# A two-model kernel on one core: the experts' head and end rearranged, and the feed-forward loops cut at another place

## The reference

```python
x = x + 0.5 * swiglu_ffn(rms_norm(x, ffn1_norm[l]), w_gate, w_up, w_down)   # d_ff 2816
...                                                                          # retention + attention
x = x + 0.5 * swiglu_ffn(rms_norm(x, ffn2_norm[l]), w_gate, w_up, w_down)
...
h = rmsnorm(x, g_ffn)                      # second block, after its mixer
g_prob = softmax(h @ w_rg + b_rg)          # 4 groups; the best one is taken
e_sel = (h @ w_re + b_re)[group]           # 8 experts in it; the best two are taken
y = sum over the two: combine * (silu(h @ w_gate[e]) * (h @ w_up[e])) @ w_down[e]
x = x + y
```

## Time and profile before

| | us |
|---|---|
| three runs | 1663.36, 1663.58, 1661.0 |
| median | 1663.36 |
| profiled execution | 1662.88 |
| its span, first to last instruction | 1661.0 |
| TensorE busy | 1503.5 |
| VectorE busy | 1006.8 |
| ScalarE busy | 701.3 |
| mean granted clock of TensorE | 0.955 |

### The profile page before, as it was taken

How to read it: one execution, slowest core, us unless ns; L and a number is a source line. 1 busy time by engine, 2 the same in 40 slices (tenths; PEclk the granted TensorE clock), 3 DMA queues, 4 the chain that set the end, 5 groups by cost and what they waited for, 6 DMA issues and landing times.

```text
span 1661.0 us, 28423 instructions
## 1 busy us (share of the span) xinstructions
PE 1503.5 (91%) x10855; PEld 1165.0 (70%) x10856; DVE 1006.8 (61%) x1859; ACT 701.3 (42%) x1211; POOL 70.1 (4%) x88
## 2 busy tenths in 40 slices
PE   8999999999999999999999999999988666666765
PEld 6888888788888888888788889888844323233322
DVE  6777788677777777787677777977643112222212
ACT  5555566455555555566455556746310000000000
POOL 1000030000001000030300000001000000000000
PEclk9999999999999999999999999999989888888788
DMA  9665363365654655363466545444889999999997
GB/s 312 202 202 177 111 240 127 102 221 184 196 183 154 212 177 193 124 239 101 144 206 202 177 152 177 154 153 149 322 353 428 429 428 428 427 428 429 429 429 320
DMA packets 152071, 407.81 MB, mean 246 GB/s; under 512 B 5568, under 2 KB 99120, under 8 KB 139344
## 3 DMA queue, kind: packets, MB, share of 16 engines
q1 hardware_dynamic: 150672, 404.28, 65.6%
q0 software_dynamic: 1344, 2.80, 0.7%
HBM read 406.00 MB, written 1.05 MB: 245 GB/s over the span
## 4 chain that ended last, share of the span: by engine, by line
PE 66%; DMA 22%; DVE 7%; ACT 3%; issue 2%; SPq 0%; DVEq 0%; ACTq 0%
DMA expert_gu<-in_exp_gu 22%; PE bank L2032 19%; PE bank L2038 10%; PE bank L1991 9%; PE bank L1992 9%; PE bank L1993 9%; PE bank L2623 3%; DVE wlo L1212 2%; ACT whi L767 1%; PE bank L2639 1%; DMA raw<-in_ffn_w_up 1%; PE bank L2576 1%; PE bank L2601 0%; DVE small L1355 0%; PE bank L2430 0%
## 5 line engine op out<-in xcount | busy, mean ns | idle before, releaser
L1212 DVE TENSOR_TENSOR wlo<-raw,whi 128x1024 fp32r<-128x1024 f32 (+1 forms) x396 | 449.6, 1183 | 80.3 <-ACT whi L767 80.2
L767 ACT ACTIVATE whi<-raw 128x1024 fp32r<-128x1024 f32 (+1 forms) x396 | 382.6, 1020 | 71.9 <-PE bank L1993 70.1
L2032 PE MATMUL bank<-hboth,whi 128*128 128x512 f32 x1408 | 350.3, 391 | 2.1 <-DVE hboth L1255 1.3
L2032 PEld LDWEIGHTS bank<-hboth,whi 128*128 128x128 f32 x1408 | 258.7, 188 | 54.0 <-ACT whi L767 2.0
L2623 PE MATMUL bank<-expert_gu,h_e 128*32 128x256 f32 x2112 | 170.1, 480 | 117.4 <-DMA expert_gu<-in_exp_gu 113.4
L2623 PEld LDWEIGHTS bank<-expert_gu,h_e 128*32 128x32 f32 x2112 | 77.0, 132 | 206.7 <-issue 117.6
L2038 PEld LDWEIGHTS bank<-hboth,wlo 128*128 128x128 f32 x1408 | 191.3, 190 | 13.1
L2038 PE MATMUL bank<-hboth,wlo 128*128 128x256 f32 x1408 | 196.0, 283 | 0.0
L1931 DVE SCALAR_TENSOR_TENSOR e_sg<-e_th,bank 128x128 f32<-128x128 f32 x33 | 9.5, 288 | 299.0 <-ACT e_th L1171 299.0
L1991 PE MATMUL bank<-whi,hboth 128*128 128x512 f32 (+2 forms) x384 | 150.3, 392 | 1.5 <-DVE hboth L1255 0.9
L1991 PE MATMUL bank<-whi,act_hi 128*128 128x512 f32 x352 | 140.1, 398 | 10.0 <-DVE act_lo L1321 10.0
(11 more groups left out here) (377 smaller groups left out, 1753.8 us busy)
## 6 DMA issues: line engine op xcount, KB each, us to landing
expert_gu<-in_exp_gu SPq DMA_DIRECT2D x62, 2048.0 KB, 40.4
expert_dn<-in_exp_dn SPq DMA_DIRECT2D x31, 2048.0 KB, 41.1
raw<-in_ffn_w_gate SPq DMA_DIRECT2D x44, 1024.0 KB, 5.5
raw<-in_ffn_w_up SPq DMA_DIRECT2D x44, 1024.0 KB, 7.5
raw<-in_ffn_w_down SPq DMA_DIRECT2D x44, 1024.0 KB, 4.9
raw<-in_w_in SPq DMA_DIRECT2D x36, 1024.0 KB, 5.2
raw<-in_w_o SPq DMA_DIRECT2D x8, 1024.0 KB, 5.4
raw<-in_w_out SPq DMA_DIRECT2D x4, 1024.0 KB, 5.0
```

The costliest lines, as they stand in the source:

```text
L767: nc.scalar.activation(slot_view(whi, slot, src), src, ACT.Copy).then_inc(hi_ready, inc)
L1212: nc.vector.tensor_tensor(slot_view(wlo, slot, src), src, slot_view(whi, slot, src).bitcast(F32), ALU.subtract).then_inc(lo_ready, inc)
L2032: nc.tensor.matmul(out_[:], wh[:, k, :], hboth[:, k, :, :], start=k == 0, stop=False, skip_group_check=True)
```

## The change

Feed-forward stages: on ScalarE and VectorE the split of a window's down weight moves from the head of the window to the end of the window before it, so the loops turn at another place; the first one stands ahead of the stage's row scale. On TensorE the row scale's two products stand ahead of the high products of window 1's gate instead of behind them. The branch for a feed-forward stage at the very end of the plan goes.

Experts' head: the router's columns become the weights and the tokens the moving data; the two halves of the result are copied to `logitsT` (one by ScalarE, one by VectorE) and turned back by TensorE. ScalarE takes over one of two copies of turned x. The norm product of the second half of x moves behind the logits' copy. `take` of the first block is made straight from the counts. The total counts go to another bank with a signal of their own. `rows(0)` and `rows(1)` move into the first block, behind its first half and ahead of its last two steps. The first three experts are written out ahead of the loop. `Y` is opened by products of the identity with x instead of zeros.

Experts' end: for experts 30 and 31 the scatters and the gather stand between the two halves of gate-up. Each bank of `Y` signals by itself, and is copied into x, two by VectorE and two by ScalarE. x is stored in four transfers instead of two.

```diff
+                for h in range(2):
+                    if not moe:
+                        sp.wait_ge(x_ready, 4 * len(stages) - 2 * (T - 1 - t))
+                    elif h == 0:
+                        sp.wait_ge(x_ready, 4 * len(plan) + t + 1)
+                    else:
+                        sp.wait_ge(xn_ready, 2 * T + t + 1)
+                    sp.dma_start(out[0, t * P:(t + 1) * P, h * 512:(h + 1) * 512], x[:, t, h * 512:(h + 1) * 512]).then_inc(stored, 16)
...
             def ffn(i):
                 st, b, m = plan[i]
                 base = 22 * kind_index(i)
-                row_scale(i)
+                def down_split(c, o, r):
+                    k = o // 2
+                    split_hi(st, (b + k) % 2, batch_value(b + k, r), 2, o % 2, m + 3 * c, m + 3 * o)
...
-                    split_hi(st, (b + k) % 2, batch_value(b + k, r), 2, o % 2, m + 3 * c, m + 3 * o, 3 if tail else 1)
...
+                    if o < 21:
+                        down_split(c + 1, o + 1, r)
+                down_split(0, 0, 0)
+                row_scale(i)
...
-                    for h in range(2 if t == 0 else 0):
+                    for h in range(2 if t == 0 else 1):
...
+                act.wait_ge(logits_done, 1)
+                nc.scalar.activation(logitsT[0:LOGITS, 0:P], bank[6][0:LOGITS, 0:P], ACT.Copy).then_inc(logits_copied, 1)
...
+                for t in range(T):
+                    act.wait_ge(y_ready, ends_of(i) + 2 * t + 2)
+                    nc.scalar.activation(x[:, t, 512:1024], Y[2 * t + 1][:], ACT.Copy).then_inc(xn_ready, 1)
...
+                def down_split(c, o):
+                    split_lo(st, (b + o // 2) % 2, 2, o % 2, m + 3 * c, m + 3 * o)
...
+                    down_split(c + 1, o + 1)
+                down_split(0, 0)
                 dve.wait_ge(rcol_ready, rcol_index(i) + 1)
...
+                dve.wait_ge(logits_done, 2)
+                V.tensor_copy(logitsT[0:LOGITS, P:S], bank[7][0:LOGITS, 0:P]).then_inc(logits_copied, 1)
+                dve.wait_ge(x_ready, 4 * i)
+                V.tensor_tensor(xn[:, 1, :], x[:, 1, :], gain[:], ALU.mult).then_inc(xn_ready, 1)
                 dve.wait_ge(root_ready, roots[0])
-                dve.wait_ge(logits_done, 1)
+                dve.wait_ge(logits_done, 3)
...
                 dve.wait_ge(counts_done, 1)
-                link(V.tensor_scalar(blocks[:, 0, :], bank[5][:, 2 * NE:3 * NE], 1.0, (BS - 1) / 2, ALU.max, ALU.add))
+                before_me = bank[5][:, 0:T * NE].rearrange("p (t n) -> p t n", t=T)
+                V.tensor_tensor(hits[:, 0:T, :], iota.rearrange("p (o s) -> p o s", o=1).broadcast_to([P, T, BS]),
+                                before_me[:, :, 0:1].broadcast_to([P, T, BS]), ALU.is_equal).then_inc(take_step, 1)
+                dve.wait_ge(take_step, 1)
+                V.tensor_tensor(take[:], hits[:, 0:T, :], both[:, :, 0:1].broadcast_to([P, T, BS]), ALU.mult).then_inc(take_ready, 1)
+                dve.wait_ge(counts_done, 2)
+                link(V.tensor_scalar(blocks[:, 0, :], bank[7][:, 0:NE], 1.0, (BS - 1) / 2, ALU.max, ALU.add))
...
-                update_x(i, 1.0)
+                for t in range(T):
+                    dve.wait_ge(y_ready, ends_of(i) + 2 * t + 1)
+                    V.tensor_copy(x[:, t, 0:512], Y[2 * t][:]).then_inc(x_ready, 1)
...
                         out_ = (G_, U_)[e][o % 2]
+                        if scale and e == 0:
+                            row_scale(i)
                         pe.wait_ge(lo_ready, mm + 1)
                         for k in range(KC):
                             high_product(out_, wh, k)
-                        if scale and e == 0:
-                            row_scale(i)
                         low_products(out_, wl, mm, 1)
...
+                        ins = nc.tensor.matmul(bank[6 + t][0:LOGITS, 0:P], w_router[:, k, :], hcol[:, k, t * P:(t + 1) * P],
+                                               start=k == 0, stop=k == KC - 1)
+                    ins.then_inc(logits_done, 1)
+                pe.wait_ge(logits_copied, 2)
+                for t in range(T):
+                    ins = nc.tensor.transpose(bank[4][:, t * LOGITS:(t + 1) * LOGITS], logitsT[0:LOGITS, t * P:(t + 1) * P],
+                                              ident[0:LOGITS, 0:LOGITS])
...
+                for t in range(T):
+                    for h in range(2):
+                        nc.tensor.matmul(Y[2 * t + h][:], ident[:], x[:, t, h * 512:(h + 1) * 512], start=True, stop=False,
+                                         skip_group_check=True)
...
+                def block_of(k, j, landed, between, first=False):
...
+                        if c == KC // 2:
+                            ins.then_inc(gu_half_done, 1)
+                            if between:
+                                scatter_and_gather(k)
+                            if first:
+                                pe.wait_ge(expout_ready, 3)
+                                pe.wait_ge(cum_ready, 1)
+                                rows(0)
+                            pe.wait_ge(gu_rest_landed[j], landed)
+                        if first and c == KC - 2:
+                            pe.wait_ge(diag_ready, 1)
+                            pe.wait_ge(rows_ready, 1)
+                            rows(1)
...
                 pe.wait_ge(cum_ready, 1)
-                with pe.Fori(0, NE // RING) as r:
+                for j in range(RING):
+                    expert(j, j, 0, first=j == 0)
+                with pe.Fori(1, NE // RING) as r:
                     for j in range(RING):
                         expert(r * RING + j, j, r)
                 for e in range(NE // RING * RING, NE):
-                    expert(e, e % RING, e // RING)
+                    expert(e, e % RING, e // RING, between=True)
```

More of the change, by code:

```diff
@@ L1322, in window @@
                                             act_hi[:, o % 2, :].bitcast(F32), ALU.subtract).then_inc(actlo_ready, 1)
-                    if tail or last and o % 2:
+                    if o == 21:
                         return
@@ L2633, in block_of @@
                     scatter(1, False).then_inc(given, 1)
+                def block_of(k, j, landed, between, first=False):
+                    pe.wait_ge(gu_landed[j], landed)
+                    pe.wait_ge(he_ready, k + 1)
+                    for c in range(KC):
+                        if c == KC // 2:
[11 more added lines that the diff above has]
+                            rows(1)
+                        for q_ in range(Q):
+                            ins = nc.tensor.matmul(bank[4][BS * q_:BS * (q_ + 1), 0:2 * P], h_e[:, c, :], expert_gu[j][:, c, q_, :],
+                                                   start=c == 0, stop=c == KC - 1, tile_position=(0, BS * q_))
+                    ins.then_inc(gu_done, 1)
+                    if not between:
+                        scatter_and_gather(k)
+                    if first:
+                        pe.wait_ge(rows_ready, 2)
                     pe.wait_ge(down_landed[j], landed)
@@ L2642, in block_of, with expert @@
                     ins.then_inc(ydown_done, 1)
-                def expert(e, j, round_):
+                def expert(e, j, round_, between=False, first=False):
                     lo = pe.value_load(cum[0:1, bass.ds(e, 1)], min_val=0, max_val=MAXB)
```

70 lines of the change are left out of this document (23 added, 47 removed).

## The result

The changed kernel takes 1647.89 us in the median of four runs (1646.27, 1646.61, 1649.96, 1649.17), the kernel before 1662.18 (1660.92 to 1663.58) beside it: a ratio of 0.9915 with a 95% interval of 0.9904 to 0.9927. The forecast was 1646.0, with a range of 1641 to 1653 that holds the result. The profiled execution took 1646.27 us, with a span of 1644.4 against 1661.0, so 16.6 us less, where the sum had 17.4. The medians are only 14.3 us apart: the profiled execution of the changed kernel is the fastest of its four, and that of the kernel before (1662.88) lies 0.7 us above its median.

What follows compares the result with a forecast made beforehand. TensorE was taken to bound the kernel up to about 1198 us, DMA engines the experts' part. Gains of 13.3 (loops), 2.5 (head) and 1.6 (end) summed to 17.4 us, giving 1646.0 us against the median 1663.36; range 1641 to 1653.

Steps and rivals of the forecast that it cites:

- Feed-forward loops: Four feed-forward stages: wait before the first down product goes, except in the first stage, and clock stays high; 13.3 us gain.
- The three signs named: Feed-forward stages: one act_lo wait of about 1.8 us, clock 1.00 over first down products, mixer's end some 13 us earlier.
- Rival (b): Feed-forward stages: the wait turns into another, second activation or a weight late; 8.9 us gain, 1654.5 us; chance 0.10.
- Rival (c): Feed-forward stages: first activation still waits because the moved down weight has not landed; 4.1 us gain, 1659.3 us; chance 0.05.
- The clock's part of the term: First down products stay at 2.4 GHz: 1.66 us each in second and fourth stage, 0.1 in third, 0 in first.
- The head: Experts' head: first block's first half done sooner, releasing the loads earlier; 2.5 us gain, between 1.4 and 4.5.
- delay only the second load, and that stays hidden behind the first load's 4.9 us: Experts' head: row products, 1 us each (2 at low clock), moved behind the first block's first half, cost nothing.
- The end: Last two experts and output: earlier down product, faster update and stores, less a slow-clock allowance; 1.6 us, bounds -0.5 and 3.0.
- The estimate that stood beside the sum: Kernel's end: with some 2 us fixed cost per transfer, smaller last store lands hardly sooner; 1.3 us, not 1.6.
- The 0.8 us subtracted for a slow last down product: Kernel's end: after idling some 3 us, the last down product might take 3.4 us instead of 1.9; about an even chance.
- (a): Experts' head gains nothing and the end's last product is slow; 13.9 us gain, 1649.5 us; chance 0.14.
- (d): Experts' head: code fetch for the written-out experts waits like a queued load, 41.1 us; slower, 1687.1 us; chance 0.03.

Runs made afterwards that it cites:

- filler products: Kernel before with three float32 products nobody reads put on TensorE ahead of the first down product of each feed-forward stage: 1657.12 us, ratio 0.9971.
- the row product later: Changed kernel with the second row product behind the first block's gate-up, VectorE waiting for the rows only at first use: 1648.31 us, ratio 0.9921.
- all three edits: Changed kernel with second half's norm product ahead of the logits wait, second row product behind gate-up, stores from two queues: 1646.92 us, ratio 0.9910.
- the undone edit: Changed kernel with the scatters and gather of the last two experts behind gate-up again: 1648.33 us, ratio 0.9918.
- the second execution of the changed kernel: Profiled execution of the unchanged changed kernel run again on another chip: 1649.98 us; median there 1649.30 us, ratio 0.9919.
- two commands: Changed kernel with x stored in two transfers, one per 128 tokens, instead of four: 1647.98 us, ratio 0.9917.
- two queues: Changed kernel with ScalarE issuing the stores of the halves it copies, SyncE the others: 1647.32 us, ratio 0.9912.

## Why the prediction was right, point by point

**Feed-forward loops: right in mechanism and size.** 13.4 us against 13.3; by stages 2.0, 4.3, 2.8 and 4.3 us against 2.4, 4.15, 2.6 and 4.15. The three signs named came: the wait for act_lo gone but for one of 1.6 us in the first stage (forecast 1.8), the clock at 1.00 over the first down products, E sooner by 13 us. Rival (b), a second wait, did not come: the second activation was late in the first stage alone, as worked out. The waits of these products on whi and wlo, a sign of being wrong, changed only from 0.7 us in all (whi) to 0.9 (0.7 of it wlo). Rival (c) did not either: ScalarE split the moved down weight without a wait for its landing. The clock's part of the term was checked by itself: filler products gained 5.1 us, and in the trace 1.6 us in the second and in the fourth stage and 0.1 in the third, against 1.66, 1.66 and 0.1 in the sum. The first stage gave 1.9 more there; the sum had rightly put 0 for it, because with the change the up weight's landing decides in that stage. That the clock fell in three stages of one execution and in four of another (the one with the experts' part alone) is what the forecast, made from one profile, could not see.

**The head: one step wrong, and the gain smaller than forecast.** The logits came 0.88 us later (forecast 0.8), the identity products took 3.70 us (forecast 3.4) and were over before the picks, and the router's products were done in 3.68 (forecast 3.5). The early take brought what it should: the half was over 3.0 us sooner than before, not the 2.5 taken. The step that failed is that the row products "delay only the second load, and that stays hidden behind the first load's 4.9 us". The second command came 4.1 us behind the first, and the DMA engines moved 369 GB/s there, not 412. That cost 1.2 us, so the term, forecast at 2.5, is 1.8 in this pair of traces and not 3.0. The runs with the row product later (last load 0.8 us sooner) and with all three edits (1.5 us sooner, 408 GB/s) show it by taking it away. Against all traces with the old head the gain is 0.9 us in the mean: the kernel before was profiled in an execution whose first block ran longer at the low clock than in any of the four others, and the sum took that block's time as fixed. The bound of 4.5 us for this term does not follow from its rows: the half was done at 1220.2 and could be at 1216.2, which is 4.0. The price of the norm product behind the copy, 0.8 us in the sum, was 0.7 where it was moved. The DMA engines' empty stretch shrank from 6.7 us to 3.7 (from 1201.4 to 1205.1), where 4 was named.

**The end: one term right, one too large, one not due; the total is near by luck.** The down product is bound by its own landing, as worked out: 0.9 us against 0.95, and the undone edit gives it back. The update and the stores were put at 1.5 us and brought 0.5. The step that failed is that the last store is issued 1.2 us sooner and its transfer is shorter: it is issued 0.5 us sooner, since four commands in one queue replace two, and from its command to its landing it takes hardly less. From the end of the last scatters to the end of the span it is 5.2 us, where 4.3 was named as a sign of being right. The estimate that stood beside the sum, with the fixed cost per transfer, had the direction right (1.3 us for the end, measured 1.4). The 0.8 us subtracted for a slow last down product was an even chance and not due in this profile (1.93 us); in the kernel with all three edits it was (3.32 us). So 1.0 us too much and 0.8 us too little made up the 1.6 that lies beside the measured 1.4: that is luck, not a right working.

**The rule on the clock gate.** The Trainium skill, TensorE: Matmul & The Clock Gate, section "HAM oscillation — how this bites in real kernels", was carried over in the prediction to mean that the last block is slow every time. The waits for DMA in that section's example are longer (3 to 5 us) than those here, so this is no test of its own case. For the waits here the traces disagree with "every time": the last down product took 1.93 us in both profiled executions of the changed kernel, though TensorE had waited 2.93 us ahead of it in the first. They agree with the direction: with all three edits it took 3.32 us after the same wait, and in the second execution of the changed kernel the first half of the last gate-up took 3.64 us after 3.04 us of waiting.

**Rivals and times.** (a) is close to what the median shows: it had 1649.5 for a head without gain and a slow end (by the sum's own terms the end would bring 0.8 us then and not 0.6, so 1649.3). The mean gain of the head in the traces is 0.9 us, executions with the low clock in the head and in the last blocks give it back, and the median of all nine is 1649.17. So the times do not settle between the forecast and this rival; the mechanism told in it, a loss ahead of the logits that eats the early take, is not what the traces show. (d), a fetch of code: the first block's start came 3.4 us sooner from E, so there was none of a size that counts. Where the sum was 17.4, the profile gave 16.6 and the medians 14.3 and 13.2. The profiles differ by more than the medians since that of the changed kernel lies 1.6 us under its median and that of the kernel before 0.7 us above. What differs between two traces of the changed kernel is the clock, and the forecast had no term for that; the range held it.

## What to carry to other kernels

When an engine's loop has a step ahead of the critical one, look at the loop's start first: cut the loop so that what the first turn does not need to wait for stands ahead of the wait, and move the producer of the awaited value ahead of other work on its engine too, since either edit alone left some 0.7 us of a wait of 2.5. Price a wait of TensorE twice, once as idle time and once as the low clock on what follows, and take both from rows. Before a term is sized against one trace of the old kernel, look at the same stretch in several: here the old head alone differed by 1.6 us between five traces. When a queue of large loads is restarted, the first command is half of the matter: the second has to follow well within the time that the first one's transfer takes, 2.9 us behind it rather than 4.1 for loads of 4.9 us here.

## What the runs showed of the hardware that was not expected

- After the same wait of 2.5 us, TensorE's granted clock fell in three of four feed-forward stages of the kernel before and in four of four with the experts' part alone, whose loops are the same. It fell inside the mixer (1056 to 1061 us, 0.66 in the mean) in one execution of the changed kernel and not in the other (1.00). One program gave times 4.9 us apart (1646.27 to 1651.15); the two that were profiled differ in the clock there, in the head and in the last blocks.
- One store command of four can take 1.44 or 1.70 us instead of 0.44; it was seen in two of the profiled executions with four commands on SyncE's queue. Why is open.
- The 1 MB of stores ended 4.3 to 4.6 us after the first command in the kernel before (1656.70 to 1661.0), the changed one (1639.95 to 1644.4), with two commands (1642.08 to 1646.4) and with two queues (1640.61 to 1645.2).
